# Banded attention branches with projections of split numbers: three products for four passes, their input split at the end of the feed-forward in front

## The reference

```python
def swa_attention(x, w_qkv, b_qkv, sinks, w_o, b_o):
    qkv = x @ w_qkv + b_qkv                      # 1024 x 1536: q 1024, k 256, v 256
    ...
    scores = einsum(q, k of this block and the one before) * 64 ** -0.5
    probs = softmax(concatenate([where(band, scores, -inf), sink]))[..., :-1]
    return einsum(probs, v) @ w_o + b_o          # 1024 x 1024
...
h = h + 0.5 * rmsnorm(swiglu(rmsnorm(h, g[0]), w_in, w_out), g[1])
h = h + rmsnorm(mixer(rmsnorm(h, g[2])), g[3])
h = h + 0.5 * rmsnorm(swiglu(rmsnorm(h, g[4]), w_in, w_out), g[5])
```

## Time and profile before

| | before |
|---|---|
| median of 3 runs | 3578.28 us (3578.1 to 3579.01) |
| profiled execution, its own time | 3576.68 us |
| its span, first to last instruction | 3575.0 us |
| PE busy | 3343.2 us |
| DVE busy | 1880.8 us |
| ACT busy | 1442.5 us |
| POOL busy | 179.6 us |
| mean granted TensorE clock | 0.968 |

### The profile page before, as it was taken

How to read it: one execution, slowest core, us unless ns; L and a number is a source line. 1 busy time by engine, 2 the same in 40 slices (tenths; PEclk the granted TensorE clock), 3 DMA queues, 4 the chain that set the end, 5 groups by cost and what they waited for, 6 DMA issues and landing times.

```text
span 3575.0 us, 48139 instructions
## 1 busy us (share of the span) xinstructions
PE 3343.2 (94%) x20670; PEld 2874.1 (80%) x20670; DVE 1880.8 (53%) x2868; ACT 1442.5 (40%) x2459; POOL 179.6 (5%) x214
## 2 busy tenths in 40 slices
PE   6998999998999989898999999989998999799897
PEld 6986998975798978586989877977877887687797
DVE  4435545544445555564555534555455556625676
ACT  3434445432344433213444434444534434324453
POOL 0000000002000000330000000000001000000100
PEclk9999999999999999999999999999998999899999
DMA  6552655544556543414565535531022334341352
GB/s 219 194 192 83 212 193 202 186 160 149 184 193 212 178 143 126 142 42 156 192 199 185 192 118 183 188 126 34 17 103 86 119 106 150 121 106 48 118 189 95
DMA packets 411217, 521.92 MB, mean 146 GB/s; under 512 B 41559, under 2 KB 353484, under 8 KB 410876
## 3 DMA queue, kind: packets, MB, share of 16 engines
q1 hardware_dynamic: 405964, 516.23, 43.8%
q0 software_dynamic: 816, 2.10, 0.2%
q10 hardware_dynamic: 4224, 0.52, 0.1%
HBM read 516.19 MB, written 2.10 MB: 145 GB/s over the span
## 4 chain that ended last, share of the span: by engine, by line
PE 86%; DVE 7%; ACT 3%; issue 1%; POOL 1%; DMA 1%; SPq 0%; POOLq 0%; DVEq 0%; ACTq 0%
PE ps L186 21%; PE ps L187 21%; PE ps L188 21%; PE ps L178 10%; PE ps L196 3%; PE ps L1176 2%; PE ps L553 1%; PE ps L3423 1%; PE ps L3420 1%; ACT a L1196 1%; POOL junk L2772 1%; DVE a L2285 0%; PE ps L1352 0%; DVE a L710 0%; PE ps L3145 0%
## 5 line engine op out<-in xcount | busy, mean ns | idle before, releaser
L186 PE MATMUL ps<-a 128*128 128x256 f32 (+1 forms) x4488 | 1425.3, 318 | 29.4 <-DVE a L710 10.6
L187 PE MATMUL ps<-a 128*128 128x256 f32 (+1 forms) x4488 | 1422.7, 317 | 0.0
L188 PE MATMUL ps<-a 128*128 128x256 f32 (+1 forms) x4488 | 1419.6, 316 | 0.0
L186 PEld LDWEIGHTS ps<-a 128*128 128x128 f32 x4488 | 865.9, 193 | 91.9 <-DVE a L710 13.5
L188 PEld LDWEIGHTS ps<-a 128*128 128x128 f32 x4488 | 864.8, 193 | 53.6
L187 PEld LDWEIGHTS ps<-a 128*128 128x128 f32 x4488 | 865.9, 193 | 51.7
L886 DVE TENSOR_TENSOR a<-ring,a 128x1024 fp32r<-128x1024 f32 x594 | 693.5, 1221 | 360.8 <-ACT a L880 360.8
L880 ACT ACTIVATE a<-ring 128x1024 fp32r<-128x1024 f32 x594 | 585.6, 1048 | 252.8 <-PE ps L188 226.8
L984 ACT ACTIVATE tmp<-ps 128x256 f32<-128x256 f32 x176 | 67.4, 383 | 510.3 <-PE ps L188 510.3
L990 DVE TENSOR_TENSOR a<-tmp,ps 128x256 f32<-128x256 f32 x176 | 74.1, 421 | 302.4 <-ACT tmp L984 302.4
L611 POOL TENSOR_TENSOR small<-small,cst 128x1 f32<-128x1 f32 (+1 forms) x78 | 51.1, 657 | 2918.9 <-DVE small L606 2030.0
(11 more groups left out here) (368 smaller groups left out, 3638.0 us busy)
## 6 DMA issues: line engine op xcount, KB each, us to landing
ring<-in_ffn_w_in_dram SPq DMA_DIRECT2D x220, 1024.0 KB, 7.3
ring<-in_ffn_w_out_dram SPq DMA_DIRECT2D x121, 1024.0 KB, 5.0
ring<-in_ada_w_dram SPq DMA_DIRECT2D x48, 1024.0 KB, 5.3
ring<-in_swa_w_qkv_dram SPq DMA_DIRECT2D x12, 1024.0 KB, 8.2
ring<-in_gla_w_in_dram SPq DMA_DIRECT2D x12, 1024.0 KB, 5.9
ring<-in_rwkv_w_rkv_dram SPq DMA_DIRECT2D x12, 1024.0 KB, 5.1
ring<-in_na_w_qkv_dram SPq DMA_DIRECT2D x12, 1024.0 KB, 5.2
ring<-in_swa_w_o_dram SPq DMA_DIRECT2D x8, 1024.0 KB, 5.0
```

The costliest lines, as they stand in the source:

```text
L186: pe.x.matmul(out, lh, rh, start=start and i == 0, stop=False)
L187: pe.x.matmul(out, lh, rl, start=False, stop=False)
L188: ins = pe.x.matmul(out, ll, rh, start=False, stop=stop and i == n - 1)
```

## The change

The two banded branches now multiply split numbers. `M.S` holds the pieces of K, Q and V (12 pieces, two buffers), `M.SO` the eight pieces of the output projection, each with a buffer of its own. The pieces 0 and 1 (all of K) and the input are split in the ending of the feed-forward in front; the pieces from 2 on are split in the branch, two ahead of PE. With the last four blocks of Q, ACT and DVE also split output pieces 0 to 3; output pieces 4 to 7 follow after the attention. The ring slots of K, Q and V are given back when DVE has split them. The meeting of all engines before the output projection is gone, the one at the branch's start stays. `pe_splitA` can wait for the input half by half. The other mixers are as before. The diff, cut to its core:

```diff
-def pe_splitA(K, pe, S, n0, key, ncols, xs, ntok, rot, out):
+def pe_splitA(K, pe, S, n0, key, ncols, xs, ntok, rot, out, fresh=None):
 
     s, (xh, xl) = K.s, xs
     for i in range(ncols // 128):
@@ -362,8 +362,13 @@
         bank, freed = rot.take(out, key, "out", i)
         pe.wait_ge(*s.dve.at("lo", S.tag, n0 + i))
         pe.wait_ge(*freed)
-        mm3(pe, bank[:, 0:ntok], [((wh[:, k, :], wl[:, k, :]), (xh[:, k, 0:ntok], xl[:, k, 0:ntok])) for k in range(8)]).then_inc(
-            *s.pe.up(key, i))
+        for half in range(2):
+            if i == 0 and fresh is not None:
+                for t in range(2):
+                    pe.wait_ge(*s.dve.at("xl", fresh, t, half))
+            ins = mm3(pe, bank[:, 0:ntok], [((wh[:, k, :], wl[:, k, :]), (xh[:, k, 0:ntok], xl[:, k, 0:ntok]))
+                                            for k in range(4 * half, 4 * half + 4)], half == 0, half == 1)
+        ins.then_inc(*s.pe.up(key, i))
         s.pe.seal("used", S.tag, n0 + i)
...
 def act_split_x(K, act, f, t, ready):
-    xh, s = K.ffn[f].xs[0], K.s
+    xh, s = K.xs[f][0], K.s
     for half in range(2):
         k = slice(4 * half, 4 * half + 4)
         act.wait_ge(*ready[half])
@@ -703,7 +708,7 @@
 
 
 def dve_split_x(K, dve, f, t):
-    (xh, xl), s = K.ffn[f].xs, K.s
+    (xh, xl), s = K.xs[f], K.s
...
-def dve_finish(K, dve, tag, src, coef, gcol, f=None, early=False, pairs=0, bias=None, piece=False):
+def dve_finish(K, dve, tag, src, coef, gcol, f=None, early=False, pairs=0, bias=None, opened=None):
 
     row, nxt = K.rows[tag, "g"], gcol is not None
     for half in range(2):
         dve_scale(K, dve, tag, 0, half, src[0], row, coef, bias)
-    if piece:
-        dve_piece(K, dve, f, "u", 0)
+    if opened is not None:
+        dve_open(K, dve, opened, 1)
...
+def opens(K, f):
+
+    return K.ffn[f].next in K.ffn
...
+    act_open(K, act, f)
+    act_finish(K, act, ("f", f), down_banks(K), down_halves(K, f), K.ffn[f].gcol is not None, K.ffn[f].next, False, 2)
...
+    nxt = K.ffn[f].next
+    if opens(K, f):
+        act.wait_ge(*K.s.pe.at("up", "u", f, NF - 2))
+        act_piece(K, act, f + 1, "g", 0)
+        act.wait_ge(*K.s.pe.at("up", "g", f, NF - 1))
+        act_piece(K, act, f + 1, "u", 0)
+    elif nxt is not None:
+        act.wait_ge(*K.s.pe.at("up", "u", f, NF - 1))
+        for n in range(2):
+            act_split_w(K, act, K.first[nxt], n, 128)
+
+
+def dve_open(K, dve, f, n):
+    nxt = K.ffn[f].next
+    if opens(K, f):
+        dve_piece(K, dve, f + 1, "gu"[n], 0)
+    elif nxt is not None:
+        dve_split_w(K, dve, K.first[nxt], n, 128)
...
+    dve_open(K, dve, f, 0)
+    dve_finish(K, dve, ("f", f), down_banks(K), 0.5, K.ffn[f].gcol, K.ffn[f].next, False, 2, None, f)
...
+def pe_split_end(K, pe, tag, S, xs, f):
+    pe_split_out(K, pe, S, tag, xs, (0, 1), 2)
+    pe_finish(K, pe, tag, True, 1)
+
+
+def act_split_end(K, act, tag, S, xs, late, f, biased=False):
+    for t in range(2):
+        act_turn_split(K, act, tag, xs, (2 * t, 2 * t + 1), t)
+    for n in range(late, 8):
+        act_split_w(K, act, S, n, 512)
+    act_piece(K, act, f, "g", 0)
+    act_piece(K, act, f, "u", 0)
+    src, ready = out_src(K, tag, biased)
+    act_finish(K, act, tag, src, ready, True, f, True, 1)
+
+
+def dve_split_end(K, dve, tag, S, xs, late, f, gcol, biased=False):
+    for t in range(2):
+        dve_turn_split(K, dve, tag, xs, (2 * t, 2 * t + 1), t)
+    for n in range(late, 8):
+        dve_split_w(K, dve, S, n, 512)
+    dve_piece(K, dve, f, "g", 0)
+    dve_piece(K, dve, f, "u", 0)
+    src, ready = out_src(K, tag, biased)
+    dve_finish(K, dve, tag, src, 1.0, gcol, f, True, 1, K.rows[tag, "b"] if biased else None)
...
-    M.xt, M.ot = K.xt3(T), v3(K.xtbuf[:, 2048:4096], T)
     M.QT, M.KT, M.V = v3(K.arena(2048), T), v3(K.arena(1024), T), v3(K.arena(512), 256)
     M.O = v3(K.arena(2048), D)
+    bufs, bufs_ = K.twin(4096)
+    out = [K.arena(1280, F32R)[:, 0:1024] for _ in range(2)]
+    parts = [K.arena(1024, F32R) for _ in range(4)]
+    M.xs = K.xs[tag] = v3(K.arena(2048, F32R), T), v3(K.fast_xt[:, 0:2048], T)
+    M.os = v3(bufs_[:, 0:2048], T), v3(K.fast_xt[:, 2048:4096], T)
+    M.S = K.first[tag] = Pieces(tag, parts[0:2], parts[2:4])
+    M.SO = Pieces((tag, "out"), out + [K.fast_gb[:, 0:1024], K.fast_gb[:, 1024:2048]] + parts)
...
+SWA_OUT = 4
+SWA_PIECES = ((0, 1024, 256), (2, 0, D), (10, 1280, 256))
+
+
+def swa_width(n):
+    return 128 if n < 10 else 256
...
-    load_cols(K, sp, (tag, "k"), w, 1024, 256, 8, (s.pe, (tag, "k", 1)))
-    sp_projA(K, sp, (tag, "q"), w, 0, D)
-    sp_projB(K, sp, (tag, "v"), w, 1280, 256, (0, 1))
-    sp_mixer_end(K, sp, tag, K.I["swa_w_o"][M.j], K.I["norm_g"][M.layer, 3], f, K.I["swa_b_o"][M.j])
+    for n, c0, m in SWA_PIECES:
+        sp_splitA(K, sp, M.S, n, w, c0, m)
+    sp_mixer_end(K, sp, tag, K.I["swa_w_o"][M.j], K.I["norm_g"][M.layer, 3], f, K.I["swa_b_o"][M.j], M.SO)
...
-    s, tag, xt = K.s, M.tag, M.xt
+    s, tag, (xh, xl) = K.s, M.tag, M.xs
     meet(K, pe, ("f", f - 1))
     K.free.clear()
     rot = Turns(K, range(3, 8))
-    c = K.w[tag, "k"]
-    pe.wait_ge(*c.landed)
-    for p in range(2):
-        bank, freed = rot.take(s.act, tag, "k", "out", p)
-        pe.wait_ge(*freed)
-        mms(pe, bank[:, 0:T], [(v3(c.buf, 256)[:, k, p * 128:(p + 1) * 128], xt[:, k, :]) for k in range(8)]).then_inc(*s.pe.up(tag, "k", p))
-    pe_projA(K, pe, (tag, "q"), D, xt, T, rot, s.act)
+    pe_splitA(K, pe, M.S, 0, (tag, "k"), 256, M.xs, T, rot, s.act, tag)
+    pe_splitA(K, pe, M.S, 2, (tag, "q"), D, M.xs, T, rot, s.act)
     pe.wait_ge(K.s_dup, 64 * (M.j + 1))
 
     def amid():
-        pe_projB(K, pe, (tag, "v"), 256, xt, (0, 1), Turns(K, (6, 7)), lambda i: s.dve)
+        rot = Turns(K, (6, 7))
+        banks = [rot.take(s.dve, (tag, "v"), "out", t) for t in range(2)]
+        for q in range(2):
+            c, raw, wh, wl = M.S.of(K, 10 + q, 256)
+            pe.wait_ge(*s.dve.at("lo", tag, 10 + q))
+            for t, (bank, freed) in enumerate(banks):
+                if q == 0:
+                    pe.wait_ge(*freed)
+                ins = mm3(pe, bank[:, 0:256], [((xh[:, 4 * q + k, tk(t)], xl[:, 4 * q + k, tk(t)]), (wh[:, k, :], wl[:, k, :]))
+                                               for k in range(4)], q == 0, q == 1)
+                ins.then_inc(*(s.pe.up((tag, "v"), t) if q else s.pe.up()))
+            s.pe.seal("used", tag, 10 + q)
...
-    pe_mixer_end(K, pe, tag, M.ot, f)
+    K.s.pe.seal("end", (tag, "core"))
+    pe_split_end(K, pe, tag, M.SO, M.os, f)
...
     meet(K, act, ("f", f - 1))
     for p in range(2):
-        act.wait_ge(*s.pe.at(tag, "k", p))
+        act_split_w(K, act, M.S, 2 + p, 128)
+        act.wait_ge(*s.pe.at((tag, "k"), p))
         for n in range(2):
             g, half = 2 * p + n, slice(n * 64, n * 64 + 64)
-            ins = act.x.activation(M.KT[half, g, :], K.place[tag, "k", "out", p][half, 0:T], AF.Identity,
+            ins = act.x.activation(M.KT[half, g, :], K.place[(tag, "k"), "out", p][half, 0:T], AF.Identity,
                                    bias=K.col("swa_b%d" % M.j, 8 + g, 1)[half])
-            ins.then_inc(*(s.act.up(tag, "k", "out", p) if n else s.act.up()))
+            ins.then_inc(*(s.act.up((tag, "k"), "out", p) if n else s.act.up()))
     for i in range(8):
+        act_split_w(K, act, M.S, 4 + i, swa_width(4 + i))
+        if i >= SWA_OUT:
+            act_split_w(K, act, M.SO, i - SWA_OUT, 512)
         act.wait_ge(*s.pe.at((tag, "q"), i))
         act.x.activation(M.QT[:, i, :], K.place[(tag, "q"), "out", i][:, 0:T], AF.Identity, bias=K.col("swa_b%d" % M.j, i, 1)).then_inc(
             *s.act.up((tag, "q"), "out", i))
     act_attention(K, act, M.A)
-    for t in range(2):
-        act_turn(K, act, tag, M.ot, (2 * t, 2 * t + 1), t)
-    act_mixer_end(K, act, tag, f, True)
+    s.act.seal("end", (tag, "core"))
+    act_split_end(K, act, tag, M.SO, M.os, 4, f, True)
...
     s, tag = K.s, M.tag
     meet(K, dve, ("f", f - 1))
+    for n in range(2, 4):
+        dve_split_w(K, dve, M.S, n, 128)
     bv, sink = K.rows[tag, "bv"], K.rows[tag, "sink"]
     dve.wait_ge(*sink.landed)
     dve.x.tensor_copy(M.sk.rearrange("p (a two m) -> p a two m", two=2, m=4),
                       sink.buf[:, 0:16].rearrange("p (a m two) -> p a two m", two=2, m=4)).then_inc(*s.dve.up(tag, "sk"))
+    for i in range(8):
+        dve_split_w(K, dve, M.S, 4 + i, swa_width(4 + i))
+        if i >= SWA_OUT:
+            dve_split_w(K, dve, M.SO, i - SWA_OUT, 512)
...
-    for t in range(2):
-        dve_turn(K, dve, tag, M.ot, (2 * t, 2 * t + 1), t)
-    dve_mixer_end(K, dve, tag, f, K.col("norm_g", M.layer * 48 + 32, 8), True)
+    s.dve.seal("end", (tag, "core"))
+    dve_split_end(K, dve, tag, M.SO, M.os, 4, f, K.col("norm_g", M.layer * 48 + 32, 8), True)
...
+            K.ffn[2 * layer].next = tag if tag in K.xs else None
...
```

(2 more changed lines are left out.)

48 lines of the change are left out of this document (19 added, 29 removed).

## The result

The change takes 3556.08 us in the median of 4 runs (3553.94 to 3559.37), the kernel before beside it 3578.19 us: a ratio of 0.9939, 95% interval 0.9921 to 0.9956, or 22 us. Run once more beside other kernels it took 3558.81 us, ratio 0.995 (0.9937 to 0.9962), 18 us. The 3558.81 us of the second measurement lie inside it. The profiled execution took 3556.76 us, 19.9 us less than that of before.

A forecast was written before the change was run, and what follows sets the result against it. TensorE's work was taken as the bound (busy 94%, 86% of the chain). Per branch 3.65 + 1.5 - 5.9 - 0.4 - 6.1 = -7.25 us, -14.5 for both: 3563.8 us, range 3557 to 3571.

The forecast's parts named there:

- Three products for four passes: K and Q: 80 products at 0.359 us, 28.7 us against 34.70, -5.9 us a branch, weight splits costed at nothing.
- The input split: Ending in front of the branch: K starts at about 13.5 us where it started at 9.83, +3.65 us (3.3 to 4.0).
- The clock at K's start: K's first products: up to 3.4 us run at half clock, taken as +1.5 us a branch, ends 0 and 3.
- V: First scores and V: between 0 and -1.25 us, taken as -0.4, since VectorE would end as late as before.
- The output projection: After the attention: 24.1 us, 4.2 us of it at half clock, against 30.2 with the wait, -6.1 us a branch.
- C: Theory formed during the experiments: TensorE's wait before the projection lengthens the half clock where it lies wholly inside it.
- No stall: Rival, Q's blocks: TensorE stands if output weights land late; 8 us a branch, 3580; 0.04 together with products no faster.
- no late transfer: Same slower rival: output weights wanted about 2084.6, landing 2092.5; it decides from 7.3 us of lateness.
- the products are as fast as said: Denies the rival that split products run no faster than four passes: 3588; 0.04 together with stalls.
- The second rival: K's start and V: the clock does not fall, V gives its whole gain; -9.6 us each, 3559; large gain 0.13.

## Why the prediction was right and wrong

- **Three products for four passes: right.** 80 products take 28.46 us at full clock, 0.356 us each (forecast 28.7). The splits of weights cost TensorE nothing: it has no wait between blocks. (34.70 - 28.7 is 6.0, not the 5.9 of the sum; 0.1 us a branch.)
- **The input split: right.** K starts at 13.39 and 13.68 us (forecast 13.5), held by the last modulation sum behind the meeting; where the meeting is moved, K starts at 12.14 and 12.67.
- **The clock at K's start: right in size for this execution** (1.5 and 1.2 us, forecast 1.5), 0 in the next. That it was right is luck: it is a draw, not a term. The Trainium skill's rule on transposes ("TensorE: Matmul & The Clock Gate", Part 4) had been read as 4.8 us at half clock and 2.1 us lost; the rows show 2.9 us at half clock in swa1, and none in the next execution.
- **V: too careful.** The forecast took -0.4 because VectorE would end as late as before; the stretch gave its whole -1.20 us, near the bound of -1.25. VectorE's delay went on from there to TensorE only for 0.15 to 0.2 us in the attention. The attention grew by 0.65 and 1.01 us, which the forecast put at nothing; the rest of that, 0.5 and 0.85 us, is half clock: 3.3 and 3.9 us of it lie in the stretch, 2.3 and 2.2 before. V gave 0.8 us a branch more than forecast and the attention cost 0.65 and 1.01 us more, so the two nearly cancel, which is luck too.
- **The output projection: the step that failed.** "It starts 0.7 us earlier, so 4.2 us lie at half clock and cost 2.1 us more: 24.1 us." It took 22.35 and 22.29 us, with 0.2 and 0 us at half clock. The 22.0 us at full clock were right to 0.3, and TensorE starts 1.0 us earlier and not 0.7, since the 16 transposes now take 3.33 us to the first product and not 3.62. The forecast took over from one execution that the half clock starts 2.3 us ahead of the attention's end and lasts 10.2 us. In the change's profile it starts 3.3 and 3.9 us ahead and lasts 6.8 us. From there it lasts 6.8 us with the wait too (all eight branches with a wait and a start 2.7 to 4.5 us ahead), so in these two branches the other start is enough to explain the miss, and the start is a draw. What the change itself does to the clock is C: without the wait, a start 1.9 to 2.5 us ahead also gives 6.8 us and at most 1.6 us inside the projection, which then takes 22.7 to 23.0 us (four branches with split products) and not 24.1. I counted the meeting's 0.73 us and not what it did to the clock. Turning and output are 2 us a branch, 4 us of the 4.9 us by which the sums differ (14.5 forecast, 19.4 in the table above).
- **The rivals.** No stall, no late transfer, and the products are as fast as said. The second rival, -9.6 us a branch or 3559, came nearest in time, in part by another way: V did give its whole gain, but the clock fell at K's start in the first profile, and the rest stood in the projection.
- **The range.** Its lower end stood on 6.3 us as the most that turning and output could give. It was 8.1 us. That the median left the range by 0.9 us, and the second measurement did not, is within what the clock's draws move.
